# Tile turns, sines and cosines made in layer 0's heads by GpSimd and ScalarE, and all four jobs of layer 1's heads with 512-column matmuls

## The reference

```python
def first_block(x, mem, norm_g, w_in, na_rpb, mem_norm_g, w_mem_kv, w_out, final_g):
    mem_n = rms_norm(mem, mem_norm_g)
    for l in range(DEPTH):
        h = rms_norm(x, norm_g[l])
        z = h @ w_in[l]
        na_q, na_k, na_v, na_g, dl_q, dl_k, dl_v, dl_g, m_q, m_g = jnp.split(z, offsets, axis=-1)
        o_na = neighbourhood_attention(..., na_rpb[l])
        o_dl = dilated_attention(rope(dl_q), rope(dl_k), dl_v)
        mk, mv = jnp.split(mem_n @ w_mem_kv[l], 2, axis=-1)
        o_m = memory_attention(m_q, mk, mv)
        y = jnp.concatenate([o_na * silu(na_g), o_dl * silu(dl_g), o_m * silu(m_g)], axis=-1)
        x = x + y @ w_out[l]
    return rms_norm(x, final_g)
```

```python
    ab_r = mag * jnp.cos(li * dt)
    ab_i = mag * jnp.sin(li * dt)
    ...
    _, _, s_r, s_i = lax.associative_scan(_complex_linear_combine, (a_r, a_i, bu_r, bu_i), axis=1)
```

## Time and profile before

| | us |
|---|---|
| median of 3 runs | 2418.33 |
| lowest, highest | 2418.19, 2419.38 |
| the profiled run | 2421.73 |
| its span | 2420.0 |
| TensorE busy | 2400.7 |
| VectorE busy | 1714.1 |
| ScalarE busy | 1218.7 |
| GpSimd busy | 526.8 |

### The profile page before, as it was taken

How to read it: one execution, slowest core, us unless ns; L and a number is a source line. 1 busy time by engine, 2 the same in 40 slices (tenths; PEclk the granted TensorE clock), 3 DMA queues, 4 the chain that set the end, 5 groups by cost and what they waited for, 6 DMA issues and landing times.

```text
span 2420.0 us, 45086 instructions
## 1 busy us (share of the span) xinstructions
PE 2400.7 (99%) x15288; PEld 2170.0 (90%) x15288; DVE 1714.1 (71%) x2644; ACT 1218.7 (50%) x1834; POOL 526.8 (22%) x1002
## 2 busy tenths in 40 slices
PE   9999999999999999999999999999999999999999
PEld 7878888998999999999999999998888888888888
DVE  8877776668888887678888876666555555555556
ACT  6444454455666665556665444444444444444442
POOL 2210032246767773210021221111000000000000
PEclk9999999999999999999999999999999999999999
DMA  7756576666666665565567777756777777777774
GB/s 253 238 177 199 187 227 202 197 195 197 192 205 210 198 197 183 184 203 188 161 196 248 257 224 232 232 193 186 199 191 191 191 191 190 190 190 192 190 190 151
DMA packets 257244, 485.07 MB, mean 200 GB/s; under 512 B 23704, under 2 KB 171876, under 8 KB 256880
## 3 DMA queue, kind: packets, MB, share of 16 engines
q1 hardware_dynamic: 216208, 415.66, 56.5%
q10 hardware_dynamic: 29632, 35.30, 4.6%
q0 software_dynamic: 11296, 32.68, 4.5%
HBM read 455.20 MB, written 31.08 MB: 201 GB/s over the span
## 4 chain that ended last, share of the span: by engine, by line
PE 82%; DVE 7%; DMA 4%; issue 3%; ACT 2%; POOL 1%; ACTq 0%; DVEq 0%; SPq 0%; POOLq 0%
PE z_ps L2233 12%; PE z_ps L2221 9%; PE z_ps L2222 9%; PE z_ps L2223 9%; PE z_ps L2649 7%; PE z_ps L2650 7%; PE z_ps L2655 7%; PE z_ps L2234 6%; DVE w_lo L1404 3%; DMA arena<-na_pad_d 1%; ACT w_hi L752 1%; DMA na_pad_d<-na_one_d 1%; DMA na_bias_d<-arena 1%; PE o_ps L2276 1%; PE s_ps L2258 1%
## 5 line engine op out<-in xcount | busy, mean ns | idle before, releaser
L1404 DVE TENSOR_TENSOR w_lo<-w_raw,w_hi 128x1024 fp32r<-128x1024 f32 x518 | 641.1, 1267 | 215.9 <-ACT w_hi L752 213.9
L752 ACT ACTIVATE w_hi<-w_raw 128x1024 fp32r<-128x1024 f32 x518 | 528.5, 1050 | 229.6 <-PE z_ps L2234 115.7
L2089 DVE TENSOR_TENSOR w_lo<-w_raw,w_hi 128x1024 fp32r<-128x1024 f32 x262 | 320.8, 1226 | 300.5 <-ACT w_hi L1244 300.5
L2233 PE MATMUL z_ps<-x_both,w_hi 128*128 128x512 f32 x1432 | 513.3, 401 | 0.7 <-DVE w_lo L1397 0.5
L1244 ACT ACTIVATE w_hi<-w_raw 128x1024 fp32r<-128x1024 f32 x262 | 277.9, 1061 | 415.3 <-PE z_ps L2655 267.8
L2234 PE MATMUL z_ps<-x_both,w_lo 128*128 128x256 f32 x1432 | 401.2, 280 | 0.0
L2221 PE MATMUL z_ps<-x_both,w_hi 128*128 128x256 f32 x1376 | 397.8, 289 | 1.1 <-DVEq L1941 0.8
L2223 PE MATMUL z_ps<-x_both,w_lo 128*128 128x256 f32 x1376 | 389.3, 283 | 0.0
L2222 PE MATMUL z_ps<-x_both,w_hi 128*128 128x256 f32 x1376 | 389.2, 283 | 0.0
L2233 PEld LDWEIGHTS z_ps<-x_both,w_hi 128*128 128x128 f32 x1432 | 269.6, 188 | 63.6 <-DVE w_lo L1397 0.8
L2649 PE MATMUL z_ps<-w_hi,x_both 128*128 128x512 f32 x704 | 275.0, 391 | 0.0
(11 more groups left out here) (474 smaller groups left out, 4186.9 us busy)
## 6 DMA issues: line engine op xcount, KB each, us to landing
w_raw<-in_w SPq DMA_DIRECT2D x624, 512.0 KB, 4.3
w_raw<-in_w SPq DMA_DIRECT2D x160, 256.0 KB, 3.3
w_raw<-in_w SPq DMA_DIRECT2D x80, 384.0 KB, 4.9
w_raw<-in_w SPq DMA_DIRECT2D x80, 128.0 KB, 3.0
tab_d<-arena ACTq DMA_DIRECT2D x32, 256.0 KB, 3.0
res<-tab_d POOLq DMA_DIRECT2D x16, 384.0 KB, 5.6
arena<-tab_d POOLq DMA_DIRECT2D x16, 384.0 KB, 6.1
tab_d<-arena ACTq DMA_DIRECT2D x32, 128.0 KB, 2.8
```

What stands on the lines that cost most here:

```text
L752: act.activation(w_hi[:, n % RING, :], w_raw[:, n % RING, :], ACT.Copy).then_inc(w_hi_ready, 1)
L1404: dve.tensor_tensor(w_lo[:, n % RING, :], w_raw[:, n % RING, :], w_hi[:, n % RING, :].bitcast(F32), ALU.subtract).then_inc(w_lo_ready, 1)
L2089: dve.tensor_tensor(w_lo[:, k % RING, :], w_raw[:, k % RING, :], w_hi[:, k % RING, :].bitcast(F32), ALU.subtract).then_inc(w_lo_ready, 1)
L2233: pe.matmul(z[:], wh, both[:, :, kt, :], start=(first and kt == kts[0]), stop=False)
```

## The change

- Turns, sines and cosines are made for four tiles at once in heads 4 to 11 of layer 0: GpSimd's `four_turns` (eight operations of 128x256) and ScalarE's `four_trigs` (four activations, a transfer of 256 KB), at the end of each of these heads. VectorE's `tile_turns` is gone. `t_vec`, the time steps, is loaded by SyncE at the start.
- Layer 1's ScalarE `tile` stores K of the tile before (`lags_store(st - 1)`, 64 KB from a single buffer `k_out`), then F, and then E from one of two buffers (128 KB). VectorE's `tile_lags(st)` waits for `k_stored` of the tile before.
- All jobs of layer 1's heads are joined.
- GpSimd's bias passes in layer 0 start before the sum of x's squares, and a pass no longer waits for its own store at its end but for the one before, after its pad.

```diff
             def tile(st, q, ...):
                 e = q % 2
                 act.wait_ge(ek_done, st + 1)
+                if not (isinstance(st, int) and st == 0):
+                    lags_store(st - 1)
                 act.dma_start(tab_d[st][:, 4 * P:TAB]..., xt[e][:, :, 1:5, :]).then_inc(f_stored[e], 16)
-                reach(act, tab_stored, 16 * st)
-                act.activation(tab_out[:, 0:2 * P], tile_bank(bank_of(st, e))[0], ACT.Copy).then_inc(e_ready, 1)
+                reach(act, tab_stored, 16 * (st - 1))
+                act.activation(e_out[e], tile_bank(bank_of(st, e))[0], ACT.Copy).then_inc(e_ready, 1)
                 ...
-                act.wait_ge(turns_ready, st + 1)
-                act.activation(tab_out[:, 3 * P + NC:4 * P], turns, ACT.Sin, scale=TURN)
-                act.activation(turn_k, turns, ACT.Sin, scale=TURN / 2).then_inc(tab_step, 1)
-                act.wait_ge(tab_step, 2 * st + 1)
+                act.wait_ge(e_ready, st + 1)
+                act.dma_start(tab_d[st][:, 0:2 * P], e_out[e]).then_inc(tab_stored, 16)
+                ...
+            def lags_store(st):
+                act.wait_ge(m_ready, st + 1)
+                act.dma_start(tab_d[st][:, 2 * P:3 * P], k_out).then_inc(k_stored, 16)
+
+            def four_trigs(j):
+                act.wait_ge(turns_ready, j + 1)
+                ...
+                act.activation(trig_out[:, :, 1, :], turns, ACT.Sin, scale=TURN)
+                act.activation(turn_k, turns, ACT.Sin, scale=TURN / 2).then_inc(tab_step, 1)
+                ...
+                act.dma_start(tab_d[bass.ds(4 * j, 4), :, 3 * P:4 * P]..., sq_sum...).then_inc(trig_stored, 16)

             def tile_lags(st, e, last=False):
                 dve.wait_ge(e_ready, st + 1)
-                reach(dve, tab_stored, 16 * st)
+                reach(dve, k_stored, 16 * st)

             def na_bias(lh):
                 ...
                 pool.wait_ge(pad_stored, 16 * lh + 16)
+                reach(pool, na_stored, 16 * lh)
                 ...
                 pool.dma_start(na_bias_d[lh], flat).then_inc(na_stored, 16)
-                pool.wait_ge(na_stored, (lh + 1) * 16)

                 def z_job(c, of_mem, wait_kt=None):
-                    if l == 0 or norm or c >= 2:
-                        pe.wait_ge(z_free, 4 * p + c + 1)
-                        job_joined(z_ps[c], p, c, m_both if of_mem else x_both, wait_kt)
-                    else:
-                        job(p, c, m_hi if of_mem else x_hi, m_lo if of_mem else x_lo, wait_kt)
+                    pe.wait_ge(z_free, 4 * p + c + 1)
+                    job_joined(z_ps[c], p, c, m_both if of_mem else x_both, wait_kt)
```

More of the change, by code:

```diff
@@ L169, in build @@
         b_in = msq.rearrange("p (r x) -> p r x", r=2)
-        turn_k, turn_d, turns = (msq_sum[:, NC * i:NC * (i + 1)] for i in range(3))
+        turn_k, turn_d, turns = (v.rearrange("p (s k) -> p s k", s=4) for v in (ns, nt, nr))
+        trig_out = sq_sum.rearrange("p a (s k) -> p (a s) k", k=NC).rearrange("p (s r) k -> p s r k", r=2)
+        e_out = [tab_out[:, T * e:T * (e + 1)] for e in range(2)]
+        k_out = msq_sum[:, NC:NC + P]
         c_in = msq_sum[:, 3 * NC:4 * NC].rearrange("p (r c) -> p r c", r=2)
@@ L283, in build @@
         y_lo_ready = sem("y_lo_ready")
-        pad_zeroed = sem("pad_zeroed")
+        k_stored = sem("k_stored")
         pad_filled = sem("pad_filled")
@@ L542, in sum_squares @@
                 pool.tensor_tensor(sq_sum[:, 0, :], sq_sum[:, 0, :], sq[:], ALU.add).then_inc(sq_summed, 1)
-            pool.wait_ge(sq_ready, CH)
-            pool.tensor_tensor(x_sq[0], x_sq[0], x_sq[1], ALU.add).then_inc(xsq_step, 1)
-            pool.wait_ge(pad_zeroed, 1)
+            pool.wait_ge(ones_ident_ready, 4)
             c0 = GRID_W - 1 - (RPB_COLS - 1) // 2
@@ L553, in _ @@
             pool.wait_ge(pad_filled, 32)
+            pool.wait_ge(sq_ready, CH)
             pool.dma_start(na_mask, ap["na_mask"]).then_inc(pad_filled, 16)
+            pool.tensor_tensor(x_sq[0], x_sq[0], x_sq[1], ALU.add).then_inc(xsq_step, 1)
             pool.wait_ge(pad_filled, 48)
@@ L611, in tile_powers, with sum_mem @@
                 times(x[:, :, 4, :], x[:, :, 3, :], xt_t[:, :, 0, :], l_r, l_i, 12)
-            for i in range(N_NA):
-                na_bias(i)
-            with pool.Fori(0, KT) as n:
+            def sum_mem(n):
                 pool.wait_ge(msq_ready, n + 1)
@@ L644, in _ @@
             pool.wait_ge(tab_stored, 16 * ST)
+            pool.wait_ge(k_stored, 16 * ST)
             pool.wait_ge(sums_ready, DEPTH + 1)
@@ L917, in head_period @@
                     mem_load(mem + 1)
+                if mem is not None:
+                    four_trigs(mem)
                 if l == 1:
                     tile(2 * h + 1, 2 * odd + 1, last, ct)
+                    if last:
+                        lags_store(ST - 1)
             def x_squares(i):
@@ L930, in _ @@
             x_squares(0)
[L931 removed]
+            act.wait_ge(consts_landed, 8 * 16)
             for l in range(DEPTH):
@@ L1512, in out_block @@
                                          op1=ALU.subtract).then_inc(x_lo_ready, 1)
[L1514 to L1523, removed]
-                                         op0=ALU.add, op1=ALU.subtract).then_inc(turn_step, 1)
-                dve.wait_ge(turn_step, 3 * st + 2)
-                dve.scalar_tensor_tensor(out=turns, in0=times_in, scalar=f_lo, in1=turn_d,
-                                         op0=ALU.mult, op1=ALU.subtract).then_inc(turn_step, 1)
-                dve.wait_ge(turn_step, 3 * st + 3)
-                dve.tensor_scalar(turns, turns, 0.5, -0.5, ALU.min, ALU.max).then_inc(turns_ready, 1)
             def tile_lags(st, e, last=False):
@@ L1619, in head_period @@
                 if not norm:
-                    if l == 1:
-                        tile_turns(2 * h + 1)
                     split_lo(p, 4)
@@ L1716, in _ @@
             dve.wait_ge(tab_stored, 16 * ST)
+            dve.wait_ge(k_stored, 16 * ST)
             for e in range(2):
```

90 lines of the change are left out of this document (58 added, 32 removed).

## The result

| | before | changed |
|---|---|---|
| median of 4 runs, us | 2418.86 | 2443.01 |
| lowest, highest | 2418.19, 2420.19 | 2442.24, 2450.69 |
| ratio to before, 95% interval | | 1.0106 (1.0086 to 1.0127) |
| the profiled run, its span | 2421.73, 2420.0 | 2450.69, 2449.0 |

The change makes the kernel 24.2 us slower. The forecast was +6.1 us, up to 2434: the sign is right, the size is not.

What follows compares the result with a forecast made beforehand. TensorE, busy 2400.7 of 2420.0 us, was taken as the bound, so only its work and waits count. Gains of 11.4 us against 17.5 lost gave +6.1, 2424.4 us; range 2405 to 2434.

Steps and rivals of the forecast that it cites:

- a weight load ahead of the store: Layer 1: K store lands at I+4.4 with the load ahead, I+2.4 with it behind; I is the old store's issue.
- a fixed cost of 2.0 us and the bytes: Skill rule for a DMA: 2.15 us for the 64 KB store; the trace agrees only for heads like 746.
- 3.1 us on TensorE and 2.3 us of waits for the bank in rotary heads: Layer 1: joining jobs saves 6.4 ns per kt in 15 heads; one reduction replacing three reads frees the bank earlier.
- Layer 1's wait: Single-buffer lags wait for the previous tile's K store, delaying VectorE's scaling and TensorE: 17.5 us lost (0 to 29).
- in the four rotary heads the lags come later, because the separate rotary reads stand ahead: 0.7 each, 2.8: Layer 1's rotary heads: the new store wait costs only 0.7 us each, 2.8 us in all.
- The first wait's cause and its end: Layer 0, head 4: ScalarE's late copy came from GpSimd's late sum; earlier bias passes win 2.9 us.
- 2.9 + 1.6 + 1.2 = 5.7: Layer 0 gain: wait for ScalarE's copy gone, wait for VectorE's scaling shortened, lower clock avoided (3.5 to 7.8).
- ends near 154: Layer 0, head 4: VectorE's chain ends some 4 us sooner, leaving TensorE about 1.3 us of wait; 1.6 won.
- if layer 0's head 4 keeps a 2.9 us wait: Sign named in advance that the term for `four_turns` is wrong.
- Rival D: Layer 0: `four_turns` and `four_trigs` as late as the old sum, only 1 us won; 2429 us; chance 0.09.
- The sign that was named for it, TensorE's busy time: If TensorE's busy time falls by less than 3 us, the joined saving is wrong.
- The first two heads of layer 1: New orders on VectorE change little there: 0.3 us won (-1.5 to 2).

Runs made afterwards that it cites:

- na_early: Kernel before with only GpSimd's layer 0 order of the change (bias passes ahead of the x_sq sum, no turns in layer 0): 2416.86 us, ratio 0.9979.
- k_early: Changed kernel, still one lags buffer, with ScalarE issuing the store of a head's last lags some 8 us earlier: 2414.43 us, ratio 0.997.
- turns_first: Changed kernel with the earlier store of a head's last lags, plus four_turns(0) on GpSimd ahead of head 4's sums: 2411.46 us, ratio 0.9955.
- two_k: Changed kernel with two buffers for the lags, so VectorE waits only for the store of the tile two before: 2414.64 us, ratio 0.9972.
- two_k_sep: Changed kernel with two lags buffers and jobs 0 and 1 of layer 1's heads separate again: 2419.77 us, ratio 0.9988.

## Why does a store of 64 KB take 3 to 5 us?

The prediction held a weight load ahead of the store to be the cause. The bias load ahead of it in its own queue was in both of its rows, and so could not be told apart. This kernel moves it behind the tile:

```diff
-                if prev:
+                if prev and not (l == 1 and not norm):
                     load_bias(g, bias_src)
...
                 if l == 1 and not norm:
                     tile(2 * h, 2 * odd, last, ct)
+                    if prev:
+                        load_bias(g, bias_src)
```

> The changed kernel with the 256 KB load of the attention bias issued behind the tile's stores, not ahead of them. Theory B (the k store lands late because bytes stand ahead of it in its own queue): in heads whose weight load also stands behind (rotary), the landing falls from 4 to 5.4 us to about 2 us, and the time falls by 8 to 20 us. Rival L (the store's landing waits for the weight load whatever its own queue holds): landings stay over 3 us, and the time falls by under 5 us.

Measured: 2426.35 us (2424.95 to 2428.2), ratio 1.0016 (1.0006 to 1.0026), which is 17 us less than the changed kernel by the medians and 22 by the ratios. The stores' time to landing from 570 to 680 us, which holds the rotary heads but the first two, in the changed kernel and in this one:

```profile
DMA to landing us min/median/max: 1.5/4.1/5.4
```

```profile
DMA to landing us min/median/max: 1.5/1.6/2.7
```

Both lines take in the stores of a head's second tile as well. The four stores that VectorE waits for took 4.1, 4.9, 5.4 and 4.2 us in the changed kernel, and take 1.6, 1.8, 1.6 and 1.6 here, and TensorE's waits there are gone. In neighbourhood and memory heads they stay: the lags still wait, ten times, 17.3 us in all.

```profile
DVE arena L1577 <- DMA tab_d<-arena: 17.3, 10, 2.5
```

What differs between the two kinds is the weight load. First the rotary head near 635 us, then the neighbourhood head near 742, SyncE's load and ScalarE's store of each:

```profile
636.06 0.33 SPq L477 DMA_DIRECT2D w_raw<-in_w  x1
...
634.94 0.34 ACTq L847 DMA_DIRECT2D tab_d<-arena  x1
```

```profile
741.80 0.33 SPq L477 DMA_DIRECT2D w_raw<-in_w  x1
...
742.34 0.34 ACTq L847 DMA_DIRECT2D tab_d<-arena  x1
```

With the weight load 1.1 us behind, the store lands in 1.6 us; with it 0.5 us ahead, in 3.4. The edit also moved the weight loads of the rotary heads, from between 0.2 us ahead and 0.4 behind the store to between 0.3 and 1.1 behind, so the pair that tells the bias load's part is the one with like places: with the weight load 0.35 us behind it, the store at 661.48 took 1.6 us here, and with it 0.40 behind and the bias load ahead, the store at 584.50 of the changed kernel took 4.1. So both have their part: a load of 512 KB ahead in another queue, and a load of 256 KB ahead in its own. With neither, 64 KB land in 1.6 to 1.8 us; with the weight load alone ahead, in 3.2 to 4.0; with both, or with the bias ahead and the weight load at the same instant (644.47 against 644.50 in the changed kernel), in 3.3 to 5.4. Theory B holds for rotary heads and L for the others, each for its half.

This also answers to the prediction's sentence on a fixed cost of 2.0 us and the bytes (the Trainium skill, "DMA: Bandwidth & Descriptors", section "Anatomy of one DMA — SWDGE (gpsimd) path"), an estimate of 2.15 us: 1.6 us for a store with nothing ahead of it is under that, and 3.3 to 5.4 in traffic far over it. The section gives its sum for transfers that GpSimd issues; ScalarE issues this one. The price of this transfer moved with its neighbours.

## How stable is the loss?

> The changed kernel once more, for its time beside the others on one chip and for a second trace: 2442 to 2451 us. If the stretches at the lower clock differ from trace to trace, this one has fewer than the four that the first shows behind the waits of layer 1, and is shorter by 1.7 us for each.

Measured: 2443.09 us (2439.07 to 2450.02). The second trace has three stretches at the lower clock in layer 1, not four, and two rotary heads without any wait (26.6 and 26.7 us where the first trace has 31.3 and 30.4). Their places, K store and then weight load:

```profile
641.53 0.34 ACTq L847 DMA_DIRECT2D tab_d<-arena  x1
...
641.82 0.33 SPq L477 DMA_DIRECT2D w_raw<-in_w  x1
```

```profile
668.42 0.36 ACTq L847 DMA_DIRECT2D tab_d<-arena  x1
...
668.88 0.33 SPq L477 DMA_DIRECT2D w_raw<-in_w  x1
```

Here the weight load came 0.29 us behind the store at 641.53, which landed in 2.3 us, and 0.46 us behind the one at 668.42, which landed in 2.1. In the first trace it came 0.03 us behind, and the store took 5.4. But the order of the two does not settle it alone: with the weight load 0.40 us behind at 584.50 in the first trace and 0.39 at 582.08 in the second, both between the two places above, the store took 4.1 and 4.2 us. With the bias load ahead and the weight load just behind, the store landed either in 2.1 to 2.3 us or in 4.1 to 5.4, and which of the two it is stays open; for a head it decides over some 4 us. That fits the spread of this kernel's runs, 11 us from 2439 to 2450, where the kernel before spreads over 5 in the same runs. That each order keeps itself from head to head, as two such heads in a row suggest, was not tried.

## Layer 0

GpSimd's order of the change alone, on the kernel before:

```diff
+            pool.wait_ge(sq_ready, CH)
             pool.dma_start(na_mask, ap["na_mask"]).then_inc(pad_filled, 16)
+            pool.tensor_tensor(x_sq[0], x_sq[0], x_sq[1], ALU.add).then_inc(xsq_step, 1)
...
                 pool.wait_ge(pad_stored, 16 * lh + 16)
+                reach(pool, na_stored, 16 * lh)
...
-                pool.wait_ge(na_stored, (lh + 1) * 16)
```

> The kernel before with GpSimd's layer 0 order of the change alone (bias passes ahead of the x_sq sum, a pass waits for the store before it and not its own), no turns in layer 0. Theory P (the passes end before ScalarE needs the sum; the losses of layer 0 in the changed kernel come from four_turns beside VectorE): faster than before by 3 to 7 us, no 7.7 us idle of ScalarE near 133. Rival S (earlier passes collide with the first heads' loads and VectorE): the first heads are later by about 2 us and the gain is 0 to 3 us.

Measured: 2416.86 us (2415.07 to 2418.28), ratio 0.9979 (0.997 to 0.9989): 5.4 us faster. Both waits of head 4 are gone from the list (the one left for the scaling is in layer 1), the one at 136 us and the one at 158, and the stretch at the lower clock with them; head 4 takes 25.2 us. So this one edit alone makes as much as the prediction gave to layer 0 with `four_turns` beside it. It has one new wait, 1.7 us at 42 us, which is taken up below. The changed kernel holds this order too, and its head 4 still takes 32 us. ScalarE there, at the end of the head, and what VectorE does meanwhile:

```profile
139.28 0.42 ACT L854 ACTIVATE arena<-arena 128x256 f32<-128x256 f32 x1 [6.30 <-POOL arena L641]
```

```profile
140.68 3.24 DVE L1391 SCALAR_TENSOR_TENSOR arena<-arena 128x32 f32<-128x32 f32 x8
```

ScalarE waits 6.3 us for `four_turns(0)`. And VectorE's eight parameter operations take 3.24 us, where they took 1.77 in na_early, with GpSimd idle at that time:

```profile
136.27 1.77 DVE L1338 SCALAR_TENSOR_TENSOR arena<-arena 128x32 f32<-128x32 f32 x8
```

Two candidates, then. The first is taken away by an order that GpSimd, idle for 22.7 us ahead of the sums, has the time for (on top of k_early):

```diff
             for j in range(KT // 2):
-                if j == 0:
-                    sum_mem(2 * j)
-                    sum_mem(2 * j + 1)
-                    four_turns(j)
-                else:
-                    four_turns(j)
-                    sum_mem(2 * j)
-                    sum_mem(2 * j + 1)
+                four_turns(j)
+                sum_mem(2 * j)
+                sum_mem(2 * j + 1)
```

> k_early (2414.4 us) with four_turns(0) on GpSimd ahead of the sums of head 4, which GpSimd waited 22.7 us for. Theory Q0 (head 4 of layer 0 loses 7 us because ScalarE waits 6.3 us at its end for GpSimd's turns, and its next splits come late): ScalarE's wait for L641 goes, the waits of TensorE at 145, 151 and 161 us fall from 5.5 us in all to under 1, no stretch at the lower clock follows, and the time falls by 5 to 7 us, to 2408 or 2409. Rival V (VectorE is slowed by the turns beside it: its eight operations of L1391 took 3.2 us, and 1.8 in the kernel before): some 2 to 3 us of waits stay, since four_turns(1) still runs beside VectorE in the next head, and the gain is 2 to 4 us.

Measured: 2411.46 us (2410.26 to 2412.7), ratio 0.9955 (0.9939 to 0.9972), the lowest median of all: 11 us under the kernel before in the same runs. ScalarE's wait is gone, and TensorE's waits at 145 and 151 us with it; of head 4's 32 us 29.8 are left. But the wait at 157 us stays at 3.4 us, and it is most of what the list still has for the scaling. Against k_early the gain is 3 us, which is V's forecast (2 to 4): the intervals of the two ratios overlap, but all four runs lie below all eight of k_early. `four_turns(1)` still runs beside VectorE.

```profile
PE p_ps L2294 <- DVE arena L1545: 4.9, 3, 3.3
```

```profile
136.87 2.70 DVE L1388 SCALAR_TENSOR_TENSOR arena<-arena 128x32 f32<-128x32 f32 x8
```

To test that, GpSimd holds `four_turns(1)` back:

```diff
             for j in range(KT // 2):
+                if j == 1:
+                    pool.wait_ge(chain_v, 45)
                 four_turns(j)
```

> turns_first (2411.5 us) with GpSimd holding back four_turns(1) until VectorE has done its parameter operations of head 4 (L1382 to L1390), so that the two don't run side by side. Theory V (VectorE's operations are slowed while GpSimd's run beside them, and the 3.4 us wait of TensorE at 157 us comes from that): the eight operations of L1388 take 1.8 us again and not 2.7, the wait at 157 us falls to about 2, and the time falls by 1 to 3 us if the clock stays up. Rival M (the wait comes from the table loads and the splits of ScalarE): the wait stays over 3 us and the time within 1 us of 2411.5.

Measured: 2412.72 us (2410.85 to 2415.14), ratio 0.9969 (0.9956 to 0.9981): no gain, and the wait at 157 us is still there, 3.7 us. The parameter operations are fast again, and the splits right behind them are slow instead, beside GpSimd's operations, which are slow as well:

```profile
136.69 1.78 DVE L1390 SCALAR_TENSOR_TENSOR arena<-arena 128x32 f32<-128x32 f32 x8
...
139.15 3.31 DVE L1457 TENSOR_TENSOR w_lo<-w_raw,w_hi 128x1024 fp32r<-128x1024 f32 x2
...
139.67 1.71 POOL L630 TENSOR_TENSOR arena<-arena,ssm_f 128x256 f32<-128x256 f32 x1
```

Two splits take 2.35 us alone, and 3.31 here; L630 takes 0.73 to 0.74 us when VectorE leaves it alone, and 1.71 here. The half of V that says that the two engines slow each other down holds; the half that says that TensorE's wait can be had back by moving it a little falls; that VectorE pays wherever it meets GpSimd in this head is my reading of the rows. Rival M was not separated from it, and what makes the wait at 157 us stays open: one more table load (1.28 us, for the switch from the sines back) stands in ScalarE's queue as well.

The same contention makes a part of a wait that no part of the prediction had, TensorE's 2.4 us at 42 us (L2286; 0.3 before). GpSimd's addition of the first bias pass has moved from 41.47 to 36.87 us, beside VectorE's rotary chain, which it hadn't met before:

```profile
36.87 1.60 POOL L576 TENSOR_TENSOR arena<-arena 128x512 f32<-128x512 f32 x1 [3.75 <-DMA arena<-na_pad_d]
...
37.32 1.43 DVE L1507 TENSOR_TENSOR arena<-arena 64x256 f32<-64x256 f32 x1
```

L1507 takes 0.42 us elsewhere, so 1.0 us comes from there. In na_early the addition (L572, 37.48 us) meets another operation of the chain, L1462, which takes 1.42 us where it takes 0.42 otherwise. The rest of the wait is the chain's own start, 1.1 us later than before, which no run explains. The kernel with the x_sq sum ahead again:

```diff
+            pool.wait_ge(sq_ready, CH)
+            pool.tensor_tensor(x_sq[0], x_sq[0], x_sq[1], ALU.add).then_inc(xsq_step, 1)
             c0 = GRID_W - 1 - (RPB_COLS - 1) // 2
...
-            pool.wait_ge(sq_ready, CH)
             pool.dma_start(na_mask, ap["na_mask"]).then_inc(pad_filled, 16)
-            pool.tensor_tensor(x_sq[0], x_sq[0], x_sq[1], ALU.add).then_inc(xsq_step, 1)
```

> turns_first with GpSimd's x_sq sum ahead of the bias passes, as in the kernel before. Theory S (the early passes make the wait of TensorE at 42 us, 1.8 against 0.45 us in the kernel before, by their transfers beside the first weights): that wait falls under 0.6 us and the time by 1 to 2 us against turns_first. Rival T (the wait comes from the earlier t_vec load or from VectorE's order): the wait stays and the times agree within 0.5 us.

Measured: 2412.42 us (2410.98 to 2413.94), no different from turns_first. The wait at 42 us is gone, so S is right on its place and T falls; that the passes' transfers did it, as S has it, is not shown, and the rows above speak for GpSimd's addition. But the passes, and `four_turns(0)` behind them, come later, and new waits of 0.6 to 0.9 us stand at 103, 129 and 143 us in its stead. Head 4 is back at 32.0 us, with a wait of 3.5 us at 158 and TensorE at its lower level for 6.8 us, from 156.9 on.

## What are the joined jobs worth?

The kernel with two buffers (two_k), with jobs 0 and 1 of layer 1's heads separate again:

```diff
+                    if l == 0 or norm or c >= 2:
                         pe.wait_ge(z_free, 4 * p + c + 1)
                         job_joined(z_ps[c], p, c, m_both if of_mem else x_both, wait_kt)
+                    else:
+                        job(p, c, m_hi if of_mem else x_hi, m_lo if of_mem else x_lo, wait_kt)
```

> The kernel with two buffers for the lags (two_k, 2414.6 us), with jobs 0 and 1 of layer 1's heads separate again. By the prediction's terms the joined jobs are worth 3.1 us on TensorE and 2.3 us of waits for the bank in rotary heads: this kernel should be 5.4 us slower, 2420. Rival J2 (the 1.36 us of reductions a head cost as much as they bring): within 1.5 us of 2414.6.

Measured: 2419.77 us (2417.96 to 2421.16), ratio 0.9988 (0.9978 to 0.9997), against 0.9972 with joined jobs: 5.1 us by the medians and 3.9 by the ratios, where 5.4 were forecast. TensorE's busy time falls by 4.8 us with joined jobs, from 2401.3 to 2396.5, with one stretch at the lower clock in each. A head takes 26.4 to 27.1 us with separate jobs and 26.0 to 26.6 with joined ones.

## Why the prediction was wrong, point by point

**Layer 1's wait: the mechanism and the place were right, one term was mis-sized.** The prediction put the lags, the queue behind them and the turn in this order, and the first lags line with its store stands in VectorE's waits as it said. For the ten neighbourhood and memory heads it gave 14.7 us. The trace has 13.1 us of waits at the turn there (each counted as what the matmul comes later than its usual pitch), 2.6 at the bank behind it (0.43 us in six heads) and 1.7 for one stretch at the lower clock: 17.4. The slack that it read from the earlier trace rows was right to some tenths, and so was the place of the weight load: ahead of the store, by 0.5 to 1.2 us, in all ten.

The step that failed is "in the four rotary heads the lags come later, because the separate rotary reads stand ahead: 0.7 each, 2.8". The trace has 9.7 us of waits at the turn in these four heads, 1.7 at the bank, and 5.1 for three stretches at the lower clock: 16.5. It went wrong in three ways. The separate reads are exactly what the change removes, so the lags don't come later by them: the slack there is 2.0 to 2.4 us, no more than the 2.2 to 2.7 of the other heads. The store was given no price of its own in a rotary head; it is 4.1 to 5.4 us there. The trace before would not have given this price either: there these heads have 2.6 to 3.5 us for L789, with the weight load 0.8 to 1.6 us behind it. The change brought the weight load to between 0.2 us ahead and 0.4 behind, and the prediction asked where it goes only for neighbourhood and memory heads. And the clock was priced in layer 0 only: a wait of 2 to 3 us costs 1.7 more where it brings the clock down, and the prediction gave its new waits no such tail.

**Layer 0: the gain was there, and the cost beside it was not.** The first wait's cause and its end were right. That na_early gains 5.4 us and the sum was 2.9 + 1.6 + 1.2 = 5.7 is luck: the sum was made for passes and turns together, and for the passes alone the same rows give 2.9 + 2.9 + 1.7 = 7.5. The step that failed is the one on `four_turns(0)`: VectorE's chain "ends near 154". `four_turns(0)` took 8 us from 131.4 to 139.3, not 6.8 to 134.3, VectorE's operations beside `four_turns(1)` were slowed, and TensorE got the chain at 161.6; it waited 1.1, 0.6 and 3.5 us. `four_turns` was priced as time on GpSimd alone. By the prediction's own sign ("if layer 0's head 4 keeps a 2.9 us wait") the term is wrong. Rival D had this right, the turns as late as the old sum; it still left a gain of 1 us, where the first stage of the trace is 2.8 us longer. The first two heads got no price for GpSimd's moved addition; they lost 1 to 3 us.

**Joined jobs.** 3.1 + 2.3 us against 3.9 to 5.1 measured: near, but the two parts are not both borne out. TensorE's own part, from the earlier trace rows, is. Of the 2.3 us at the bank, from the earlier trace rows, the kernel with separate jobs has only 0.8 left (0.6 at 562 us, 0.2 at 616), so most of these waits went by another edit of the change; VectorE's lighter load is the likely one, and was not tried. The sign that was named for it, TensorE's busy time, misleads in the changed kernel: it rises by 8.2 us there, with five more stretches at the lower clock, in which the same matmuls take longer.

**The first two heads of layer 1.** 0.3 us were given, and 2.8 came (36.3 to 33.5 us). The kernel with separate jobs has 33.5 there as well, so it isn't the joined form; the cause is open.

**Why the range failed.** Its upper end, 2434, was made of 2 us a head. The bounds of the unknown cost were in the text (29 us when all stores land late), and the range did not reach to them; with them it would have ended near 2436, and the rest is layer 0 and the tail at the lower clock.

| term | forecast | measured, from |
|---|---|---|
| layer 0's passes | -5.7 | -5.4, na_early |
| `four_turns(0)` and its neighbours | in the above | +6.7, first stage of two_k against na_early |
| joined jobs | -5.4 | -3.9 to -5.1, two_k_sep |
| first heads of layer 1 | -0.3 | -2.8, stages |
| K store, ten heads | +14.7 | +17.4, first trace |
| K store, four rotary heads | +2.8 | +16.5, first trace |

The right column adds up to 27 to 29 us, against 29.0 between the two spans; the medians are 24.2 apart.

## What to carry to other kernels

A store whose completion gates the next use of a buffer should be issued soon after its data is ready, not where its code happens to stand: here eight microseconds earlier in the same queue were worth 28 to 32 us. Price a transfer with the loads that stand around it at that very place, in each kind of stage where it occurs, and give each new wait of the engine that sets the time its tail at the lower clock. Work that is moved to GpSimd is not free for VectorE: look which of its operations run beside it.

## What the runs showed of the hardware

- A K store of 64 KB landed in 1.5 to 1.6 us in most places with no load ahead of it (but in 3.0 at 592.92 and 2.6 at 741.88 in the changed kernel, why is open), and in 3.3 to 5.4 us with a 256 KB load ahead in its own queue and a 512 KB load ahead or at the same instant in another.
- With the large load issued just behind it, the small store landed at two quite different times: in 5.4 us with 0.03 us between them, 2.3 with 0.29, 4.1 with 0.40 and 2.1 with 0.46. The gap alone does not tell which.
- The GpSimd and VectorE operations here slow each other while they run side by side: eight small VectorE operations took 3.24 us beside `four_turns` and 1.77 without; two splits 3.31 and 2.35; a GpSimd multiplication 1.71 and 0.73.
- At waits of 1.4 to 3.5 us TensorE ran at the lower level for 3.4 us in several places (6.8 us in two traces), and at others of the same length it did not (2.9 us at 136 in the kernel before, 1.7 at 882 in the changed one); what decides was not settled.
